# Attention in 64x64 corners of TensorE, with diagonal matrices that transpose and scale

## What is computed

```
s_c = einsum('bgrqd,bgcd->bgrqc', qb, kc) * scale
p_c = masked_softmax(s_c, cmp_end[None, :] <= t[:, None])
o_c = einsum('bgrqc,bgcd->bgrqd', p_c, vc)
...
s_s = einsum('bgrqd,bgqkd->bgrqk', qb, ks) * scale
p_s = masked_softmax(s_s, pos_s <= t[:, None])
o_s = einsum('bgrqk,bgqkd->bgrqd', p_s, vs)
...
p_w = masked_softmax(s_w, (pos_w[None, :] >= 0) & (rel >= 0) & (rel < WINDOW))
o_w = einsum('bgrqk,bgkd->bgrqd', p_w, vw)
return gb[..., 0:1] * o_c + gb[..., 1:2] * o_s + gb[..., 2:3] * o_w
```

## Time and profile before

| | us |
|---|---|
| median of three runs | 2514.84 |
| lowest, highest | 2512.34, 2515.33 |
| span of the profiled execution | 2509.2 |
| stage `attend_and_recur` in it | 1066 to 1520, 454 |
| PE, DVE, ACT, POOL busy in the stage | 442.4, 378.9, 274.3, 94.1 |

### The profile page before, as it was taken

How to read it: one execution, slowest core, us unless ns; L and a number is a source line. 1 busy time by engine, 2 the same in 40 slices (tenths; PEclk the granted TensorE clock), 3 DMA queues, 4 the chain that set the end, 5 groups by cost and what they waited for, 6 DMA issues and landing times. The chain is left out here.

```text
span 2509.2 us, 47304 instructions
## 1 busy us (share of the span) xinstructions
PE 2471.1 (98%) x19440; PEld 2024.9 (81%) x19440; DVE 1723.1 (69%) x2720; ACT 1052.3 (42%) x1827; POOL 94.9 (4%) x146
## 2 busy tenths in 40 slices
PE   8999999999999999999999999999999999999999
PEld 7888888888887778977888787877788888888887
DVE  6976676688655464589888788634468776676676
ACT  4322223345443343466655564523343322223443
POOL 0000000000000000021231110000000000000000
PEclk9999999999999999999999999999999999999999
DMA  4223323654442258932211116501222413326464
GB/s 152 96 89 121 120 73 121 239 185 150 130 136 64 96 175 253 258 95 53 53 46 44 45 45 221 178 21 34 68 76 87 136 67 121 118 74 218 139 200 148
DMA packets 279268, 297.78 MB, mean 119 GB/s; under 512 B 75442, under 2 KB 209712, under 8 KB 279088
## 3 DMA queue, kind: packets, MB, share of 16 engines
q1 hardware_dynamic: 278080, 294.29, 37.4%
q10 hardware_dynamic: 1008, 0.92, 0.1%
HBM read 208.54 MB, written 81.36 MB: 116 GB/s over the span
## 5 line engine op out<-in xcount | busy, mean ns | idle before, releaser
L1246 PE MATMUL f_ps<-hi,f_wh 128*128 128x512 f32 x656 | 255.6, 390 | 0.8 <-DVE f_wl L930 0.8
L1248 PE MATMUL f_ps<-hi,f_wl 128*128 128x512 f32 x656 | 255.2, 389 | 0.0
L2859 PE MATMUL f_ps<-hi,f_ahead_h 128*128 128x512 f32 x384 | 160.0, 417 | 0.8 <-PEq L72 0.8
L1246 PE MATMUL f_ps<-f_t3h,f_t2h 128*128 128x512 f32 x392 | 152.5, 389 | 0.0
L1247 PE MATMUL f_ps<-f_t3l,f_t2h 128*128 128x512 f32 x392 | 152.5, 389 | 0.0
L1248 PE MATMUL f_ps<-f_t3h,f_t2l 128*128 128x512 f32 x392 | 152.5, 389 | 0.0
L2861 PE MATMUL f_ps<-hi,f_ahead_l 128*128 128x512 f32 x384 | 149.9, 390 | 0.0
L2860 PE MATMUL f_ps<-one_lo,f_ahead_h 128*128 128x512 f32 x384 | 149.8, 390 | 0.0
L1246 PEld LDWEIGHTS f_ps<-hi,f_wh 128*128 128x128 f32 x656 | 123.1, 188 | 27.2 <-issue 1.6
L1248 PEld LDWEIGHTS f_ps<-hi,f_wl 128*128 128x128 f32 x656 | 123.1, 188 | 25.6
L1247 PE MATMUL f_ps<-one_lo,f_wh 128*128 128x512 f32 x344 | 133.8, 389 | 0.0
(11 more groups left out here) (636 smaller groups left out, 6609.9 us busy)
## 6 DMA issues: line engine op xcount, KB each, us to landing
act<-one_y SPq DMA_DIRECT2D x30, 512.0 KB, 3.6
f_work<-act SPq DMA_DIRECT2D x30, 512.0 KB, 3.5
act<-y SPq DMA_DIRECT2D x30, 512.0 KB, 3.6
arena<-act SPq DMA_DIRECT2D x30, 512.0 KB, 3.7
one_y<-in_w_in SPq DMA_DIRECT2D x25, 512.0 KB, 4.0
early<-in_ffn_w_gate SPq DMA_DIRECT2D x11, 1024.0 KB, 6.2
early<-in_ffn_w_up SPq DMA_DIRECT2D x11, 1024.0 KB, 8.7
f_raw<-in_ffn_w_gate SPq DMA_DIRECT2D x10, 1024.0 KB, 6.3
```

The costliest lines, as they stand in the source:

```text
L1246: nc.tensor.matmul(out, wh, xh, start=start, stop=False)
L1248: return nc.tensor.matmul(out, wl, xh, start=False, stop=stop)
L2859: nc.tensor.matmul(dense_ps[:, b, cols], w_hi[:, b, k, :], hi[:, k, cols], start=(k == 0), stop=False)
```

## The change

**Scores.** Queries, keys and compressed keys stay fp32 and are not split (`rot` takes the place of `rot_hi` and `rot_lo`; the copy and the subtraction that made the parts, L3145 and L3313, are gone). A step is now 64 queries of both heads (`half = s % 2`) over all keys of a branch. Keys of even blocks of 64 lie on rows 0 to 63, of odd blocks on rows 64 to 127. A score is four products, one in each corner, each over `m` blocks of 64 keys (`span`); the compressed keys take two more.

**Transposes.** DVE no longer scales probabilities. It makes the reciprocal (`share`), and POOL makes from it, the gate and an identity a 64x64 diagonal per head on its rows (`diag`, 192 instructions in all). A block of 64 keys of 64 queries of both heads is turned by two fp32 products with these diagonals, `out = prob^T x diag`, which scales as well. They use the two crossed corners.

**Values.** Two products per block of 64 keys, for one or both halves of the queries, in the two straight corners. `bank` and `values` are one event, `turn`: the transposes of a fill and the values of the fill before it are written in turn, two by two. There are 136 fills of up to eight blocks (`packed`). Selected values lie in `hi`, and each half of the rows holds all values, so they are loaded twice. `fold` on POOL now makes the square too. `tiling` knows only whole and corners.

```diff
-                        nc.tensor.matmul(at, q[:, ring, 0, head % 4, :], keys, start=True, stop=False)
-                        mm = nc.tensor.matmul(at, q[:, ring, 1, head % 4, :], keys, start=False, stop=True)
+                for r, c in CORNERS:
+                    mm = nc.tensor.matmul(s_ps[rows(c), r, 0:m * CH], query(r, c), keys[k // 2][rows(r), g, at * CH:(at + m) * CH], start=True, stop=True)
...
-                        mm = nc.tensor.transpose(t_ps[:, 2 * m + h, :], src, ident[:])
+                    for a_ in range(2):
+                        mm = nc.tensor.matmul(t_ps[rows(1 - a_), x, :], src[rows(a_), col:col + CH], diag[rows(a_), u % 2, half, br, :],
+                                              start=True, stop=True)
...
-                        mm = nc.tensor.matmul(o_ps[rows(h), u % 2, :], val, probT[:, n % 2, 2 * m + h, :],
-                                              start=(f == 0 and m == 0), stop=(br == 0))
+                    for r in range(2):
+                        mm = nc.tensor.matmul(o_ps[rows(r), 0, cols:cols + n_cols], val[rows(r)],
+                                              probT[rows(r), (n - 1) % 2, x:x + len(halves)].rearrange("p x q -> p (x q)"),
+                                              start=(fv == 0 and x == 0), stop=(br == 0))
...
-                nc.vector.tensor_scalar(slot[:, 0:cols], slot[:, 0:cols], coef[:, s % 8, 1:2], None, ALU.mult).then_inc(scaled, 1)
+                        nc.gpsimd.tensor_scalar(diag[:, u % 2, half, br, :], unit[:], by, gate_rows[:, i, half, u % PAIRS, br:br + 1],
+                                                ALU.mult, ALU.mult).then_inc(weighted, 1)
...
-        return e[0] == "values" and "columns" or e[0] == "rw" and (e[2] != "var" or not crossed(e[1])) and "corners" or "whole"
+        return "whole" if e[0] == "tile" or e[0] == "rw" and e[2] == "var" and crossed(e[1]) else "corners"
```

More of the change, by code:

```diff
@@ L1590, in joint_plan @@
[L1590 to L1604, removed]
+        u, m, extra = s // 4, span(s)[1], 0.2 * (s % 4 >= 2)
@@ new lines, in joint_plan @@
+        us = 0.001 * CH * len(key_columns(s))
+        event(("score", s), "pe", 0.11 * m + 0.03 + 0.5 * extra, s and ("max", s - 1))
+        event(("max", s), "dve", 0.3 + 0.14 * m + extra, ("score", s), u >= 2 and ("turn", FIRST_FILL[u - 1] - 1))
+        event(("exp", s), "act", 0.4 + us + 2 * extra, ("max", s), s and ("exp", s - 1))
+        event(("share", s), "dve", 0.16, ("exp", s), s and ("share", s - 1))
+        event(("diag", s), "pool", 0.3 + 1.5 * extra, ("share", s), s and ("diag", s - 1))
@@ new lines, in joint_plan @@
+    for n in range(len(FILLS) + 1):
+        before = turns(FILLS[n - 1][0])[FILLS[n - 1][1]] if n else []
+        fill = turns(FILLS[n][0])[FILLS[n][1]] if n < len(FILLS) else []
+        last = n and FILLS[n - 1]
+        event(("turn", n), "pe", 0.11 * max(width(fill), width(before)), fill and ("diag", last_step(*FILLS[n])), n and ("copy", n - 1),
+              n and last[1] == 0 and last[0] and ("finish", last[0] - 1))
+        if fill:
+            event(("copy", n), "act" if n % 2 else "dve", 0.13 + 0.066 * width(fill), ("turn", n))
@@ L1749, in attend_and_recur @@
     with core.stage() as ctx:
-        ks, kw = hi[:, 0:2, :], hi[:, 2:4, :]
+        keys = [keys_of(hi, branch) for branch in range(2)]
+        vs = [hi[:, at, col:col + P].bitcast(F32) for at, col in VALUES_AT]
         q = queries_of(hi)
@@ L1973, in turn_probs, with turn @@
+                if k >= 2:
+                    for c in range(2):
+                        mm = nc.tensor.matmul(s_ps[rows(c), 0, HALF - CH:HALF], query(0, c), kc[rows(0), g, :], start=True, stop=True)
+                mm.then_inc(scored, 1)
+            def turn(n):
+                now = before = []
+                if n < len(FILLS):
+                    u, f = FILLS[n]
+                    now = turns(u)[f]
+                    pe.wait_ge(weighted, steps_through(last_step(u, f)))
                 if n:
+                    v, fv = FILLS[n - 1]
+                    before = turns(v)[fv]
@@ new lines, in turn @@
+                given, taken = 0, 0
+                ahead = [(br, half, col, x + k) for br, _, halves, x in now for k, (half, col) in enumerate(halves)]
+                while given < len(ahead) or taken < len(before):
+                    if given < len(ahead) and (taken == len(before) or given <= before[taken][3]):
+                        mm = probs(*ahead[given])
+                        given += 1
+                        if given == len(ahead):
+                            mm.then_inc(flipped, 1)
+                    else:
+                        mm = values(*before[taken])
+                        taken += 1
+                        if taken == len(before):
+                            mm.then_inc(summed, 1)
@@ L2114, in _ @@
                     score(e[1])
-                elif e[0] == "bank":
-                    turn_probs(e[1])
-                elif e[0] == "values":
-                    values(e[1])
+                elif e[0] == "turn":
+                    turn(e[1])
                 elif e[0] == "tile":
@@ L2197, in _ @@
             act.wait_ge(table_in, 1)
+            for half in range(2):
+                for c in range(2):
+                    src = gates[rows(half)].rearrange("p i (q h b) -> p i q h b", q=PAIRS, h=2)[:, :, :, 1 - c, :]
+                    nc.scalar.copy(gate_rows[rows(c), :, half], src).then_inc(gates_set, 1)
             for e in plan:
```

400 lines of the change are left out of this document (211 added, 189 removed).

## The result

| | before | after |
|---|---|---|
| median, us | 2513.59 (2510.27 to 2515.33, 4 runs) | 2544.41 (2542.69 to 2546.09, 4 runs) |
| ratio, with its 95% interval | | 1.0126 (1.0112 to 1.0141) |
| span of the profiled execution | 2509.2 | 2541.5 |
| mixer in it: first product to the first product behind it | 1066.2 to 1520.4, 454.2 | 1069.1 to 1552.9, 483.8 |

The forecast was 2456 us, with 2424 to 2495 as its range; it is wrong in sign. The mixer should have fallen to 395 us and rose to 484. Nothing outside it moved by more than 3 us.

The account below looks back on a forecast made before the run. PE's list was taken to bound the kernel; in the mixer, 337 us of array work, 4 of turn-arounds and 54 of waits made 395 us instead of 454, 59 us less, so 2456 us, with a range of 2424 to 2495.

Parts of the forecast that it names:

- The price of a product: PE in the mixer: four fp32 products of 64 columns, one in each corner, take 0.116 us.
- Array work: PE's products and transposes in the mixer: 337 us after the change, 5 more than the 332 before.
- turn-arounds: PE's changes of tiling in the mixer, 0.145 us each: 529 before, 77 us; 28 after, 4 us; 73 us less.
- 54 us of waits: PE's remaining waits in the mixer, let grow from 45 to 54 us, with ends at 22 and 93.
- scores of before: Score products of the old mixer, 528 blocks of 128 keys and the compressed keys: together 61 us of array work.
- list falls from 409 to 341 us: PE's array work plus turn-arounds in the mixer, from 409 to 341 us, still the longest list of any engine.
- my case: Whole kernel: waits of 36 to 80 us in the mixer, 2438 to 2482 us, middle 2456; 50%.
- The diagonal: Making one 64x64 diagonal on POOL: 0.33 us taken, ends 0.20 and 0.77; 192 of them, 63 us.
- The bank limit: Rival: pairs of `turn` in mixed sizes go one after the other, 127 us more, 2583 us; 3%.
- POOL's queue: Rival: diagonals stand behind up to seven products with masks on POOL and stop PE, 86 us, 2542 us; 6%.
- The room comes back as waits: Rival: chains set the mixer's pace, not PE's list; waits 80 to 100 us, 2482 to 2502 us; 22%.
- DVE's relief pays as well: Rival: less DVE work shortens PE's waits in the mixer to 20 to 35 us, 2422 to 2437 us; 19%.

Follow-up runs that it names:

- merged kernel: Changed kernel with the recurrence's products of two neighbouring pairs merged into one of twice the moving columns, its values left wrong: 2455.64 us, mixer 396.9 us.
- run 0: First series of the supply kernel, 1400 fp32 products of 64 columns in the four corners, no waits inside: 0.0283 us a record over all.
- supply kernel: A kernel of its own, computing nothing of the reference: five series of fp32 products on PE without waits, a rest before each; no total time given.
- run 4: Last series of the supply kernel, 1400 products of 64 columns in the corners; the transfers meant for it came ahead; 0.106 us a pass at clock 0.50.

## Why the prediction was wrong

*The price of a product.* 0.116 us per four products of 64 columns was right, and `turn` ran at it. But I read it off groups of at most 72 records, and used it for 15520. A packet of instructions is 127 records, longer than any row that I read. It is the array's price over a burst, not PE's over a stage.

*The sum.* Array work of 337 us and turn-arounds of 4 have nothing against them: `turn` ran at its price, 27 changes of shape came for 28, and the merged kernel, which has the same columns, ends where the forecast did, 2455.6 us with a mixer of 397 us, for 2456 and 395. That it comes so near is in part luck. 397 - 341 = 56 us look like my 54 us of waits, but 26 of them are holes at the ends of blocks of instructions (29 less the pace), so some 30 are left for waits on other engines, if the 341 hold. The change itself says the same: 484 - 341 = 143 us, 110 of them such holes, 33 left. I had let this term grow from 45 to 54, and it shrank.

*A slip that changes little.* By its own price, 0.23 us per 512 columns, the scores of before are 60.7 us without the compressed keys and 64 with them, where the sum has 61. The waits of before are then 42 us and not 45; the forecast of the change does not use the 61.

*The step that failed* is that the sum has the array, turn-arounds and waits for other engines as its only terms, as if PE had its instructions for nothing. I said that PE's "list falls from 409 to 341 us" and called its records "two" to a product, without asking what 5392 more of them need: 15520 / 127 x 3.9 = 477 us of fetches, above every other list. In the change PE stood for 110 us at the ends of its blocks of instructions, a term that my sum has at nothing. The gain of the turn-arounds was real, and the new bound took it and 30 us more. The fifty per cent for my case, and all of the 90% for faster, rested on this.

*Could it be seen blind?* In part. 80 packets in 454 us stood in the trace of before, the shortest distance between two 3.47 us; that times 122 is 423 us, more than the 395 forecast. It is a bound that I could have put beside the sum; it wouldn't have given the sign. What spoke most clearly was the count of instructions, which grew by half in a stage that was full.

*A rule beside it.* PE stood still for 1.4 to 1.9 us at every 128th record in run 0 of the supply kernel, and PE's idle time with releaser "issue" in the change is of this kind. The Trainium skill, "Runtime: NRT & Kernel Launch", section "Instruction fetch mechanics", has the 16 KiB blocks of 256 instructions, and the trace agrees with these (128 records of two instructions); it calls the cost of crossing a block "mostly hidden", and there the traces disagree wherever a block holds less than some 3.7 us of work. They agree in the kernel before, where a packet came every 5.40 us at the median and the steps at the ends of the blocks sum to 4 us.

*DVE, ACT, POOL.* 267, 260 and 173 us were forecast, 264, 260 and 175 came. The diagonal's 0.399 us lay between its ends, the squares and folds took 0.41 and 0.46.

*The rivals.* The bank limit did not come, as the 0.11 us steps show. POOL's queue gives 2542 us in the text, nearly the time measured, and is still wrong: without a single diagonal on POOL the time was no shorter. A right number from a wrong mechanism; only the run could tell. "The room comes back as waits" (80 to 100 us) didn't happen either: on other engines PE waited for some 30 us. That is what "DVE's relief pays as well" had for this term, 20 to 35 us, but its time, 2422 to 2437 us, missed by over 100, for the same lack as mine.

## What to carry to other kernels

Small tiles of TensorE trade its time for instructions. Before cutting products into 64x64 corners, count the records: 128 fp32 passes need a block of instructions, and one came per 3.5 to 4.0 us here, so a stretch whose passes cost the array less than 0.029 us each on average is bound by the fetches, whatever the array could do. A price read off a burst holds for as long as the burst; read it also over several hundred records. And look in the profile for idle time with the releaser "issue" inside a group of one line, and count PE's instructions from one such hole to the next: here it was 256 each time, one packet of the instruction queue.

## What the runs showed of the hardware that I had not expected

- The supply of instructions is a bound of its own on TensorE: 128 records at a time, 3.45 to 4.00 us a block in a kernel with nothing else, 3.9 in the mixer. After a rest of 27 us, 255 records went through in run 4 before the first hole, with the first packet beginning to move 4.0 us after their start: two blocks had lain ready.
- A wait for something long past costs TensorE's sequencer 0.06 us. 2280 of them, 137 us at that price, cost the kernel before 22 us; most of it lay beside PE's work.
- At the clock of 0.50 four corners took 0.106 us a pass of 64 columns, where they take 0.058 at the full one. Two products of 64 rows and 128 columns took 0.213 us, as long as two passes over the corners; a change of shape added some 0.2 us in all.
